# Half thirds in twelve stretches, values and sample weights turned first: the attention stage of a two-layer hybrid decoder step

## What is computed

```python
q, k, v = qkv_split(xn_p, w_qkv[i])
att = dilated_attention_prompt(q, k, v, slopes)   # branches (128,1), (512,4), (2048,16)
yp = att.reshape(...) @ w_o[i]
...
s = einsum(q, k) / sqrt(64) - slope * distance    # masked to each branch's positions
p = exp(s - m); o = p @ v / sum(p)
...
att_s = dilated_attention_sample(qs, kc, vc, buf_len, slopes)   # 4 new queries, 2048 cached keys
```

## Time and profile before

| | us |
|---|---|
| median of 3 runs | 2540.76 |
| lowest, highest | 2536.05, 2540.83 |
| the profiled execution | 2545.21 |
| its span, first to last instruction | 2543.4 |

### The profile page before, as it was taken

The page is one execution under the profiler, slowest core; times in us unless marked ns, Lnnn a source line. Parts: engine busy times, 40 slices in busy tenths (PEclk is TensorE's granted clock), DMA queues, the critical chain, the costliest instruction groups (busy, mean ns, idle before and its releaser), DMA issues.

```text
span 2543.4 us, 41675 instructions
## 1 busy us (share of the span) xinstructions
PE 2498.6 (98%) x17126; PEld 2380.1 (94%) x17126; DVE 1615.8 (64%) x2416; ACT 806.3 (32%) x1438; POOL 971.6 (38%) x664
## 2 busy tenths in 40 slices
PE   8999999999999999999999999999999999999998
PEld 8989998999999999997888888888999999999998
DVE  6999778666666655555555555555766666665556
ACT  5111344333333211143333343343433333332112
POOL 1000135777777522240010111133377777762223
PEclk9999999999999999999999999999999999999999
DMA  4111102455444443543454545433187777785222
GB/s 148 50 35 40 50 20 67 145 144 144 143 143 142 180 153 125 181 184 133 158 174 155 161 149 177 159 113 138 34 275 272 273 272 272 274 312 187 87 82 86
DMA packets 108668, 383.93 MB, mean 151 GB/s; under 512 B 24000, under 2 KB 44352, under 8 KB 106048
## 3 DMA queue, kind: packets, MB, share of 16 engines
q1 hardware_dynamic: 108480, 381.26, 44.7%
HBM read 339.15 MB, written 176.04 MB: 203 GB/s over the span
## 4 chain that ended last, share of the span: by engine, by line
PE 88%; DVE 5%; POOL 2%; DMA 2%; issue 2%; ACT 1%; SPq 0%; DVEq 0%; POOLq 0%; ACTq 0%
PE reg L1006 28%; PE reg L857 18%; PE reg L1121 10%; PE reg L824 9%; PE reg L1143 3%; PE reg L1086 3%; PE ob L1006 3%; PE reg L1157 3%; PE reg L930 2%; PE reg L837 2%; PE reg L1070 1%; POOL wq L1833 1%; PE reg L1213 1%; PE reg L1200 1%; DVE xo L2162 1%
## 5 line engine op out<-in xcount | busy, mean ns | idle before, releaser
L1006 PE MATMUL reg<-xo,wq 128*128 128x352 f32 x5280 | 862.8, 324 | 11.7 <-DVE wq L2210 3.6
L1006 PEld LDWEIGHTS reg<-xo,wq 128*128 128x128 f32 x5280 | 852.1, 189 | 15.7 <-issue 6.7
L857 PE MATMUL reg<-hid,w_sp 128*128 128x352 f32 x3024 | 485.6, 322 | 0.4 <-DVE h L1972 0.4
L857 PEld LDWEIGHTS reg<-hid,w_sp 128*128 128x128 f32 x3024 | 485.0, 188 | 0.7 <-DVE h L1972 0.7
L518 POOL TENSOR_TENSOR w_sp<-w_raw,w_sp 128x1024 fp32r<-128x1024 f32 x63 | 174.2, 2767 | 709.9 <-ACT w_sp L513 689.5
L1972 DVE TENSOR_TENSOR h<-reg,h 128x1056 f32<-128x1056 f32 x192 | 241.3, 1257 | 238.9 <-PE reg L857 210.1
L1833 POOL TENSOR_TENSOR wq<-wqr,wq 128x512 fp32r<-128x512 f32 x168 | 240.3, 1441 | 213.6 <-DVE wqr L2201 130.4
L1121 PE MATMUL reg<-xs,w_sp 128*128 128x352 f32 x1701 | 308.6, 330 | 0.0
L1833 POOL TENSOR_TENSOR wq<-w_raw,wq 128x512 fp32r<-128x512 f32 x168 | 267.8, 1607 | 56.9 <-ACT wq L1377 56.9
L1121 PEld LDWEIGHTS reg<-xs,w_sp 128*128 128x128 f32 x1701 | 269.9, 189 | 13.9 <-issue 12.6
L824 PE MATMUL reg<-xs,w_sp 128*128 128x352 f32 x1512 | 243.9, 323 | 4.5 <-DVE h L1972 4.5
(11 more groups left out here) (261 smaller groups left out, 3090.4 us busy)
## 6 DMA issues: line engine op xcount, KB each, us to landing
w_raw<-in_wstream SPq DMA_DIRECT2D x192, 512.0 KB, 4.3
out_sv<-in_cache_v SPq DMA_DIRECT2D x16, 4088.0 KB, 16.9
out_sk<-in_cache_k SPq DMA_DIRECT2D x16, 4088.0 KB, 17.2
kvr<-in_kva SPq DMA_DIRECT2D x16, 2048.0 KB, 9.4
kvr<-in_kvb SPq DMA_DIRECT2D x16, 1536.0 KB, 6.9
hid_spill<-tmp SPq DMA_DIRECT2D x44, 528.0 KB, 5.4
hraw<-hid_spill SPq DMA_DIRECT2D x44, 528.0 KB, 4.5
wt<-in_wtab SPq DMA_DIRECT2D x16, 512.0 KB, 4.0
```

Of the source, the lines that this page charges most:

```text
L857: mm = nc.tensor.matmul(out[:, t, :], w[:, wh, kk * 512 + m * P:kk * 512 + (m + 1) * P], hid[:, par_g, kk, xh, t * TS:(t + 1) * TS], start ...
L1006: mm = nc.tensor.matmul(out, w[:, wh, k * P:(k + 1) * P], xo[:, o, 1 - xh if o == X_T3 else xh, k, :], start=(first and k == 0 and wh + xh ...
```

## The change

In each group the filler between the low turn and the scores is taken out. The eighteen half thirds are put in two places of a group, twelve in all: `LEAD`, ahead of the low turn, and `COVER`, between the high turn and the weigh, one or two half thirds in each. The turn of the values (group 0) and that of the sample weights (group 3) are moved ahead of the lead, so in `TA_ORDER` and `TB_ORDER` they come ahead of the low turn, and DVE's and ACT's copies of them come ahead of the low copies. DVE takes a third behind the low copy, or behind the next scores, depending on where its second half now ends; the last third of a pair is taken ahead of the next pair's first norms. In the last pair the division differs: group 0 has no lead. There ACT's split of the last of the three output weights is moved ahead of the low copy of group 3, and a copy in group 2 is chained.

```diff
--- before.py
+++ after.py
@@ -114,11 +114,11 @@
 SAMPLE_AT = {0: 1, 1: 2, 3: 3, 4: 4}
 TA_ORDER, TB_ORDER = [], []
 for _g in range(NGR):
-    TA_ORDER.append(("lo", _g))
-    TB_ORDER.append(("lo", _g))
     if _g in (0, 3):
         TA_ORDER.append(({0: "values", 3: "weights"}[_g], 0))
         TB_ORDER.append(({0: "values", 3: "weights"}[_g], 0))
+    TA_ORDER.append(("lo", _g))
+    TB_ORDER.append(("lo", _g))
     if _g == NGR - 1:
         TA_ORDER.append(("sample", 0))
     TA_ORDER.append(("hi", _g))
@@ -141,6 +141,8 @@
 WO_FILL = (U_WO, U_WO + 1, U_WO + 3)
 ATT_THIRDS = [(t, m) for t in range(NT) for m in range(KD - 1)] + [(2, KD - 1), (0, KD - 1), (1, KD - 1)]
 NAT = NT * (KD - 1)
+LEAD = (((0, 1), (3,), (6, 7), (9,), (12, 13), (15,)), ((), (2, 3), (6, 7), (10, 11), (14,), (16,)))
+COVER = (((2,), (4, 5), (8,), (10, 11), (14,), (16, 17)), ((0, 1), (4, 5), (8, 9), (12, 13), (15,), (17,)))
 
 
 def neg_at(g, hh, n):
@@ -1221,12 +1223,13 @@
                     mm.then_inc(ta_full, 1)
 
                 for g in range(NGR):
-                    turn(g, "lo")
-                    filler(3 * g)
                     if g == 0:
                         turn_values()
                     if g == 3:
                         turn_weights()
+                    for f in LEAD[pr.last][g]:
+                        filler(f)
+                    turn(g, "lo")
                     if g < NGR - 1:
                         scores(pr, g + 1)
                     else:
@@ -1235,11 +1238,11 @@
                             pe.wait_ge(d_free, pr.n(9 + 6, 9))
                             scores(Pair(pr.p + 1), 0)
                     turn(g, "hi")
-                    filler(3 * g + 1)
+                    for f in COVER[pr.last][g]:
+                        filler(f)
                     weigh(g)
                     if g in SAMPLE_AT:
                         sample_phase(SAMPLE_AT[g])
-                    filler(3 * g + 2)
 
             pairs(pair)
 
@@ -1699,6 +1702,14 @@
                 for g in range(NGR):
                     probs(g)
                     if g == 0:
+                        act.wait_ge(tb_full, pr.n(tb("values") + 1, NTB))
+                        nc.scalar.activation(vrow[:, 4:8, :], TP[1].rearrange("p (t c) -> p t c", c=P),
+                                             ACT.Copy).then_inc(tb_free, 1)
+                    if g == 3:
+                        act.wait_ge(tb_full, pr.n(tb("weights") + 1, NTB))
+                        nc.scalar.activation(spT[:, 4:8, :], TP[1].rearrange("p (t r) -> p t r", r=P),
+                                             ACT.Copy).then_inc(tb_free, 1)
+                    if g == 0:
                         if pr.p > 0:
                             outputs(Pair(pr.p - 1), 0)
                         if not pr.last:
@@ -1709,6 +1720,8 @@
                             split_hi(act, U_WO + 1)
                     if pr.last and g in (1, 2):
                         att_split(7 * g + 4, 7 * g + 7)
+                    if pr.last and g == 3:
+                        split_hi(act, U_WO + 3, done=9 * NPAIR + 5)
                     if g == 2:
                         act.wait_ge(sp_neg, pr.n(1, 1))
                         nc.scalar.activation(sps[:, 0:NKEYS], sps[:, 0:NKEYS], ACT.Exp, bias=snm[:, 2:3], scale=-1.0,
@@ -1721,14 +1734,6 @@
                     turned(g, "lo")
                     if pr.p == NPAIR - 2 and g == NGR - 1:
                         att_split(0, 6)
-                    if g == 0:
-                        act.wait_ge(tb_full, pr.n(tb("values") + 1, NTB))
-                        nc.scalar.activation(vrow[:, 4:8, :], TP[1].rearrange("p (t c) -> p t c", c=P),
-                                             ACT.Copy).then_inc(tb_free, 1)
-                    if g == 3:
-                        act.wait_ge(tb_full, pr.n(tb("weights") + 1, NTB))
-                        nc.scalar.activation(spT[:, 4:8, :], TP[1].rearrange("p (t r) -> p t r", r=P),
-                                             ACT.Copy).then_inc(tb_free, 1)
                     if g == NGR - 1:
                         act.wait_ge(ta_full, pr.n(ta("sample") + 1, NTA))
                         for hh in range(2):
@@ -1757,9 +1762,8 @@
                     if pr.last and g == 2:
                         act.wait_ge(w_lo, cnt(U_WO))
                         act.wait_ge(ta_full, pr.n(ta("phase", 2) + 1, NTA))
-                        nc.scalar.activation(wo7[:, :, :], w_sp[:, U_WO % 3, :, (KD - 1) * P:KD * P].bitcast(F32), ACT.Copy)
-                    if pr.last and g == 3:
-                        split_hi(act, U_WO + 3, done=9 * NPAIR + 5)
+                        chain(nc.scalar.activation(wo7[:, :, :], w_sp[:, U_WO % 3, :, (KD - 1) * P:KD * P].bitcast(F32),
+                                                   ACT.Copy))
 
             first = Pair(0)
             act.wait_ge(zero_ok, 1)
@@ -2505,13 +2509,10 @@
                         nc.vector.tensor_reduce(snm[:, 2:3], snm[:, 0:2], mybir.AxisListType.X, ALU.min).then_inc(sp_neg, 1)
 
                 for g in range(NGR):
+                    if g == 0:
+                        next_third(-1)
                     for hh in range(2):
                         norm(g, hh)
-                    if g % 2 == 0:
-                        next_third(3 * g // 2 - 1)
-                    turned(g, "lo")
-                    if g % 2 == 1:
-                        next_third(3 * g // 2)
                     if g == 0:
                         dve.wait_ge(ta_full, pr.n(ta("values") + 1, NTA))
                         nc.vector.tensor_copy(vrow[:, 0:4, :],
@@ -2520,13 +2521,16 @@
                         dve.wait_ge(ta_full, pr.n(ta("weights") + 1, NTA))
                         nc.vector.tensor_copy(spT[:, 0:4, :],
                                               TP[0].rearrange("p (t r) -> p t r", r=P)).then_inc(ta_free, 1)
+                    turned(g, "lo")
+                    if LEAD[pr.last][g] and LEAD[pr.last][g][-1] % 2 == 1:
+                        next_third(LEAD[pr.last][g][-1] // 2)
                     turned(g, "hi")
                     if g < NGR - 1:
                         neg_scores(pr, g + 1)
                     elif not pr.last:
                         neg_scores(Pair(pr.p + 1), 0)
-                    if g % 2 == 0:
-                        next_third((3 * g + 1) // 2)
+                    if g < NGR - 1 and COVER[pr.last][g][-1] % 2 == 1:
+                        next_third(COVER[pr.last][g][-1] // 2)
                     if g < 2:
                         sample_scores(g)
                     if g == 2:
```

## The result

| | before | after |
|---|---|---|
| median (runs), us | 2537.45 (22) | 2542.43 (22) |
| lowest, highest | 2531.47, 2546.15 | 2537.41, 2550.28 |
| the profiled execution, its span | 2545.21, 2543.4 | 2545.72, 2543.9 |

The ratio is 1.002 (95%: 1.0011 to 1.0028): about 5 us slower, where 3.2 us were forecast. What the change did is read stretch by stretch.

What follows compares the result with a forecast made beforehand. PE, never idle in a steady pair, was taken to bound the kernel. Seven pairs +5.9, start -4.2, pair 6 +1.0 and last pair +0.5 make +3.2 us on the median 2540.76: 2544.0 us, range 2535.5 to 2549.5.

Steps and rivals of the forecast that it cites:

- Steps 1 to 4: Per steady pair: fewer stretches 0.15 and longer leads 0.39 us gained; wait for weights 1.07 and for outputs 0.32 us lost.
- step 3: Sample weights' turn behind group 2's weigh: PE waits 1.07 us per pair for DVE's multiplication, which meets POOL's split.
- Rival (a): Sample weights' turn: multiplication and POOL's split don't meet, weights ready in time; 7.5 us less, 2536.5 us; chance 0.12.
- Step 5: High turns, with low copies under the scores alone: no cost, 0.3 us of cover left for ACT.
- rival (c): Groups 2 to 4: high turns wait for the low copies, slower at 2553.5 us; chance 0.13.
- Step 6: Start of pair 0: values turned early, norms free of POOL's split, clock full; 4.2 us gained once.
- Step 7: Pair 6: the high turn waits for ACT's sample copies, 1.0 us lost once.
- Step 8: Last pair: waits in groups 1 and 2 covered, new waits elsewhere; together 0.5 us lost (bounds -1.5 and +2).
- Rivals (b) and (d): (b): only the start's gain counts, 2536.5 or 2539 us, chance 0.12; (d): no effect on time, 2541 us, chance 0.05.

Runs made afterwards that it cites:

- Experiment 2: The changed kernel with ACT's third split of the next pair's weights, and so POOL's, moved from group 2 to group 3: ratio 0.9994 to the kernel before.
- experiment 3: The changed kernel with half third 15 put back between group 5's low turn and the outputs' turn, in all pairs but the last: ratio 1.0009.
- experiment 5: The changed kernel with the edits of experiment 2, experiment 3 and experiment 4, but half third 0 ahead of the last pair's first low turn: ratio 0.9968, 2530.33 us.
- experiment 6: The kernel before with ACT's first split for the next pair moved behind the low copy, in pair 0 alone: ratio 0.9991.
- experiment 9: The changed kernel with POOL's second weight split behind the attention held back until DVE's multiply-subtract of the same column is done: ratio 0.9999.
- experiment 4: The changed kernel with the last pair's half thirds and ACT's split of the last output weights placed as in the kernel before: ratio 1.0025.
- experiment 10: The changed kernel with the edits of experiment 2, experiment 3 and experiment 9: ratio 0.9968, 2532.24 us.

## Why the prediction was right, and where it was not

**Steps 1 to 4** were right in sign and size: 0.84 us a pair forecast, 0.86 measured. The weights wait 1.07 us (start to start 1.27 against 0.20 where nothing waits) in seven pairs and hardly in the last (0.24), the outputs 0.32 us in all eight. Among the signs the multiplication was to last 1.7 us still; it lasts 2.12, as step 3's own sum implies, since it is issued earlier and ends with POOL. Experiment 2 showed the cause of the first, experiment 3 the second, and experiment 5 the gain that they covered, 0.54 us. **Rival (a)** described what experiment 2 brought about: 7.6 us, where it gave 7.5. The Trainium skill, SBUF — State Buffer, section "Who interferes with whom", was weighed there: the first to be issued of such a pair keeps the other out. The traces agree on who goes first: 0.70 against 2.12 us here, 0.57 against 2.66 us at the seam. That it waits for the other's whole instruction they show only roughly: it ends 0.49 us behind POOL's end and lasts 0.70 alone.

**Step 5** held in the steady pairs: no high turn in the changed kernel waited for a low copy, and **rival (c)** did not come about.

**Step 6** held: 4.2 us, with the clock at full. **Step 7** held: pair 6's high turn waits 1.04 us for the sample copies, 1.0 forecast. **Step 8** was a little too high. (Its wait of 0.92 us was not the only one on DVE in the last pair of the kernel before: in mid-turn of group 1 PE is idle for 0.62 us.) The low turn behind the values waits 1.0 us from start to start, 1.2 forecast,

```profile
1659.50 1.06 PE L1145 MATMUL reg<-ident,neg_s 128*128 128x128 f32 x8 [0.76 <-DVE vrow L2518]
```

and the row behind the last weigh waits 0.90 us for ACT's copy of the outputs:

```profile
1726.21 0.73 PE L1253 MATMUL reg<-xs,w_sp 128*128 128x352 f32 x3 [0.90 <-ACT att L1669]
```

but with the other terms as measured (7 x 0.86 - 4.2 + 1.0 = +2.8) the last pair is worth -0.2 us, not +0.5, of the +2.6 of attention. **Rivals (b) and (d)** fall with the 73.36 us.

**What was missing** is the seam, 2.9 of the 5.5 us; the sum had it at nothing. The sum stopped at the end of the pairs: step 8 followed PE to the last weigh and priced the half third that left from there by what it hid ahead of `last_row`. That half third was also time for the loads of `h` and of the next weights. Against PE's start on `U_WO + 2`, ACT's next split begins at +8.48 us instead of +6.78, since the load lands later:

```profile
1738.06 1.06 ACT L513 ACTIVATE w_sp<-w_raw 128x1024 fp32r<-128x1024 f32 x1 [4.37 <-DMA w_raw<-in_wstream]
```

```profile
1739.00 1.06 ACT L515 ACTIVATE w_sp<-w_raw 128x1024 fp32r<-128x1024 f32 x1 [6.07 <-DMA w_raw<-in_wstream]
```

Everything on ACT, POOL and DVE behind it is later by the same 1.7 us, up to the addition on which PE waits. In both profiles POOL's split went first, so between them this shift makes the 1.6 us of waiting, and the lower clock the other 1.3. With DVE first in both, the old last pair (experiment 6) idles 1.47 us and the new one (experiment 9) 2.94: the same shift again, by the traces; no run moved the load alone, so this part of the seam is read, not tested. On top of it comes the order: a tie in the kernel before, so that some of its runs can have the short form, and POOL ahead by 0.35 us in the changed one. Experiment 9 shows that this order costs 2.5 us of idle time and 1.3 us of clock. Why the load is issued 1.35 us later against PE (0.70 us ahead of its start, before 2.05) the code and the traces tell together. In SP's queue it stands behind five loads of `h`, and these wait for DVE's second addition of the partial outputs (`part_used`). The addition ends 5.19 us ahead of PE's start before and 3.82 after, and SP issues 0.08 us later both times (timelines of DVE and SP, before and then after):

```profile
1724.84 1.25 DVE L2569 TENSOR_TENSOR h<-h,KT 128x1056 f32<-128x1056 f32 x1
...
1726.17 2.48 SPq L783 DMA_DIRECT2D h<-h_spill  x5
```

```profile
1724.28 1.26 DVE L2573 TENSOR_TENSOR h<-h,QT 128x1056 f32<-128x1056 f32 x1 [0.40 <-DMA h<-h_spill]
...
1726.79 2.33 SPq L785 DMA_DIRECT2D h<-h_spill  x5
```

Of the 1.37 us, 0.40 are DVE waiting for the rows of `h` loaded behind sample phase 4; for the rest, by the order of PE's queue, PE comes sooner, with no half third left behind the last weigh. The sentence "no queue of DMAs moves against its consumer" was wrong for the loads behind the pairs, and so was its reason for the last pair: there two half thirds stand between the third and the fourth sample phase, not three, and the load between them has 7.18 us instead of 8.71 (it lands 0.49 us ahead of its use).

How often the kernel before takes either order at the seam was not measured, so the share of the seam in the timed 5 us isn't exact. The mean granted clock of an execution gives a hint: it is 0.996 or 0.997 in 35 of the 83 executions of the kernel before that ran beside the experiments, in 10 of 11 of experiment 6, and in 4 of 22 of the changed kernel.

**Luck** has a part in the number. The forecast for the median, 2544.0, lies 1.6 us above the measured 2542.43. It built on a median of three executions that was 3.3 us above that of the 22 (2540.76, 2537.45), while the change was 1.8 us larger than forecast: the two errors partly cancel.

## What to carry to other kernels

Before a cover is moved, ask for each operation that stood behind it what the other engines do at its new time: a wait of 1 us in a loop of seven costs more than what was gained at two places, and the cure was to move the other engine's work by one group. Follow the edit past the end of the loop, to the next place where the engine that sets the time waits, and look there for instructions of DVE and GpSimd that are issued within a fraction of a microsecond of each other: pin their order with a wait. Where a cover stands between a load's issue and its use, moving it moves the load's slack: 7.67 us were not always enough for a load of 6.5 to 9.2 us. Then compare stretches start to start, not spans.

## What the runs showed of the hardware

Two things had not been expected. **The feed-forward loop has two paces.** The same ten columns of 132 matmuls, with PE busy throughout at the full clock, take 212.67 us in the profile of the changed kernel and 209.73 us in that of experiment 4, with the same code:

```profile
1950.84:2163.51 212.67, 212.67 (x1322) 212.67 (x1322) 132.93 (x191) 66.38 (x120) 153.20 (x120) 1.00 0.78 273
```

```profile
1945.65:2155.38 209.73, 209.73 (x1322) 209.73 (x1321) 133.05 (x191) 66.42 (x120) 153.44 (x121) 1.00 0.78 277
```

That is 21.27 or 20.97 us a column, held over most of a loop of twenty, so up to 6 us per loop, and by that size it can be a large part of the scatter between executions. From the 1000th matmul behind the seam to the end of the span, seven of the twelve profiles take 628 to 629 us and five 623 to 624. What sets the pace was not found.

**The clock's answer to idle time is not graded by its length alone.** Behind 1.42 us of idle time (start, after) it stayed at 2.4 GHz, behind 2.28 us (start, experiment 6) it fell to 1.2 GHz, behind 2.59 us (seam, experiment 10) it stayed, behind 2.94 us (experiment 9) and 3.84 us (before) it fell for 3.4 us, behind 5.45 us for some 6 us. The Trainium skill, TensorE: Matmul & The Clock Gate, section "Part 1: The HAM clock gate", says that the clock is set by how busy the engine has been recently; no run here tells what else than the idle time decided between 2.28 and 2.59 us.
